# The fourth picked tile's v rows: one slot per fetch, tokens on partitions, summed by DVE

## The reference, cut to what matters

```
def peer_apply(h, expert, gate, u_tab, v_tab):
    # by blocks of tokens: h (n, 1024), expert and gate (n, 8, 16), tables (16384, 1024)
    ub = take(u_tab, expert)                  # one u row for each token and slot
    vb = take(v_tab, expert)                  # one v row for each token and slot
    a  = gelu(einsum('nd,nhkd->nhk', h, ub))  # 128 dot products a token
    return einsum('nhk,nhkd->nd', gate * a, vb)
# block(): x = x + gate2 * peer_apply(...), then a final rmsnorm with g_final
```

## Time and profile before

| | |
|---|---|
| time, median of 3 runs | 3561.27 us (3556.86 to 3562.12) |
| time of the profiled execution | 3564.63 us |
| its span, first to last instruction | 3563.0 us |
| mean granted TensorE clock | 0.949 |
| PE busy | 3114.4 us, 87% |
| DVE busy | 2311.0 us, 65% |
| POOL busy | 1446.0 us, 41% |
| ACT busy | 904.1 us, 25% |
| mixing on PE (L1742) in the chain that ended last | 7% |

### The profile page before, as it was taken

The page is one execution under the profiler, slowest core; times in us unless marked ns, Lnnn a source line. Parts: engine busy times, 40 slices in busy tenths (PEclk is TensorE's granted clock), DMA queues, the critical chain, the costliest instruction groups (busy, mean ns, idle before and its releaser), DMA issues.

```text
span 3563.0 us, 46587 instructions
## 1 busy us (share of the span) xinstructions
PE 3114.4 (87%) x17171; PEld 2346.7 (66%) x17171; DVE 2311.0 (65%) x4881; ACT 904.1 (25%) x1256; POOL 1446.0 (41%) x1188
## 2 busy tenths in 40 slices
PE   8899969444677557999999999999999999999996
PEld 1466634222454446888887888888888888888884
DVE  1233218999988976777776777776777775444445
ACT  0111111000666782222222122222222222221222
POOL 0001001555444556555554555555545543222224
PEclk9999989777899888999999999999999999999998
DMA  9611242666121329999998999999999997655654
GB/s 359 174 60 67 72 157 94 229 225 224 73 101 78 159 118 357 336 334 324 337 331 314 335 326 336 335 322 335 341 325 337 329 328 258 213 195 208 212 199 177
DMA packets 305763, 858.03 MB, mean 241 GB/s; under 512 B 25360, under 2 KB 108816, under 8 KB 303840
## 3 DMA queue, kind: packets, MB, share of 16 engines
q0 software_dynamic: 151344, 551.09, 43.0%
q1 hardware_dynamic: 154189, 305.27, 24.8%
q10 hardware_dynamic: 108, 0.22, 0.0%
HBM read 793.34 MB, written 63.15 MB: 240 GB/s over the span
## 4 chain that ended last, share of the span: by engine, by line
PE 59%; POOL 1%; issue 1%; DVE 1%; DMA 0%; ACT 0%; DVEq 0%
PE y_ps L1724 25%; PE a_ps L1705 24%; PE picked_ps L1742 7%; PE uT_ps L1692 3%; POOL shared L1446 0%; POOL rstd_d L1450 0%; DMA shared<-in_peer_u,ids 0%; POOL shared L1398 0%; POOL quad L1408 0%; DMA quad<-in_peer_v,idsT 0%; DVE h_lo L1640 0%; POOL quad L1446 0%; DVE uT_lo L1528 0%; DVE quad L1652 0%; DVE shared L1569 0%
## 5 line engine op out<-in xcount | busy, mean ns | idle before, releaser
L1408 POOL DMA_INDIRECT quad<-in_peer_v,idsT x512 | 533.4, 1042 | 518.2 <-PE picked_ps L1742 367.5
L1398 POOL DMA_INDIRECT shared<-in_peer_u,ids x384 | 444.5, 1158 | 640.5 <-DVE acts L1569 593.0
L1557 DVE TENSOR_TENSOR shared<-shared,y_ps 128x512 f32<-128x512 f32 x640 | 439.2, 687 | 340.2 <-PE y_ps L1724 312.1
L1705 PE MATMUL a_ps<-h_hi,uT_lo 128*128 128x320 f32 x2048 | 643.1, 314 | 1.7 <-DVE h_lo L1640 1.7
L1705 PE MATMUL a_ps<-h_hi,uT_hi 128*128 128x320 f32 x2048 | 633.1, 309 | 0.0
L1705 PE MATMUL a_ps<-h_lo,uT_hi 128*128 128x320 f32 x2048 | 633.1, 309 | 0.0
L1724 PE MATMUL y_ps<-v_hi,m_lo 128*128 128x512 f32 x1280 | 510.7, 399 | 11.0 <-DVE shared L1557 8.5
L1724 PE MATMUL y_ps<-v_lo,m_hi 128*128 128x512 f32 x1280 | 504.3, 394 | 0.0
L1724 PE MATMUL y_ps<-v_hi,m_hi 128*128 128x512 f32 x1280 | 501.6, 392 | 0.0
L1569 DVE CUSTOM_DVE_ANT_0 shared<-shared 128x1024 f32<-128x1024 f32 x384 | 464.6, 1219 | 22.3 <-DMA shared<-in_peer_u,ids 17.2
L1705 PEld LDWEIGHTS a_ps<-h_hi,uT_lo 128*128 128x128 f32 x2048 | 385.3, 188 | 7.2 <-issue 2.1
(11 more groups left out here) (172 smaller groups left out, 4220.1 us busy)
## 6 DMA issues: line engine op xcount, KB each, us to landing
shared<-in_peer_u SPq DMA_DIRECT2D x128, 512.0 KB
v_all<-in_peer_v SPq DMA_DIRECT2D x128, 512.0 KB
gate_blocks<-dense SPq DMA_DIRECT2D x10, 4096.0 KB, 11.7
gates<-gate_blocks SPq DMA_DIRECT2D x64, 640.0 KB
w_ada<-in_w_ada SPq DMA_DIRECT2D x12, 2048.0 KB, 11.0
x_in<-in_x_prompt SPq DMA_DIRECT2D x16, 512.0 KB, 4.1
quad<-in_peer_v,idsT POOLq DMA_INDIRECT x512
shared<-in_w_in SPq DMA_DIRECT2D x8, 768.0 KB, 12.5
```

Of the source, the lines that this page charges most:

```text
L1398: pool.indirect_dma_start(out=rows[n % 4], out_offset=None, in_=u_table, in_offset=bass.IndirectOffsetOnAxis(ap=ids[:, t, slot:slot + 1], ...
L1408: pool.indirect_dma_start(out=quads[half][q], out_offset=None, in_=v_table, in_offset=bass.IndirectOffsetOnAxis(ap=idsT[:, t, token:token ...
L1557: nc.vector.tensor_tensor(part, part, y_ps[n % RING][:, :], ALU.add).then_inc(S.y_free, 1)
L1705: last = nc.tensor.matmul(a_ps[n][:, 0:GROUP], lhs[s][:, k, :], rhs[:, k, tok], start=k == 0 and m == 0, stop=k == KD - 1 and m == 2)
```

## The change

For tile 3 alone (MIXED = 3 tiles are mixed as before) the v rows are fetched like the u rows: one slot of 128 tokens at a time, tokens on partitions, into the ring of four. DVE multiplies each by its token's weight (a column of mT, not transposed) and adds it to a sum in SBUF (add_row). POOL fetches no tokens and PE mixes nothing in the last quarter. ACT takes gelu from acts without PE's transpose, and the gates of tile 3 are kept untransposed in routing. FINAL becomes 0 to 8 in order. The buffers of the tail lie elsewhere, so that SP loads g_final, gate2, the three sums and the first two x1 tiles before the dense work is over.

```diff
--- before.py
+++ after.py
@@ -17,6 +17,7 @@
...
 PICKED = 4
+MIXED = PICKED - 1
@@ -876,7 +877,11 @@
                 act.wait_ge(S.slotsT_ps, t + 1)
                 nc.scalar.activation(idsT[:, t, :], x_ps[:, 0, :], ACT.Copy).then_inc(S.slotsT, 1)
-                nc.scalar.activation(gatesT[:, t, :], x_ps[:, 2, :], ACT.Copy).then_inc(S.slotsT, 1)
+                if t < MIXED:
+                    nc.scalar.activation(gatesT[:, t, :], x_ps[:, 2, :], ACT.Copy).then_inc(S.slotsT, 1)
+                else:
+                    nc.scalar.activation(gatesT[:, t, :], slots[:, 2, :, :].rearrange("p h k -> p (h k)"), ACT.Copy)\
+                        .then_inc(S.slotsT, 1)
             def left_rows(d, b):
@@ -1239,6 +1244,8 @@
     SEGMENT = PAIRS // PICKED
     PER_PAIR = P // SEGMENT
     DOTS = (PICKED - 1) * P
+    ROWS = DOTS + P
+    MIXED_PAIRS = MIXED * SEGMENT
     with ExitStack() as mem:
         ff, u, token_row, rows = expert_memory(shared)
         ids, idsT, gatesT, acts = picks
@@ -1263,20 +1270,20 @@
         mean = sbuf(nc, mem, "mean_d", [P, TILES])
         rstd = sbuf(nc, mem, "rstd_d", [P, TILES])
         h_raw = [ff[:, t, :] for t in range(DENSE)]
-        sums = quads[1][0]
-
-
-        x1 = [u[0], u[1], rows[0], rows[1]]
-        g_last = rows[2]
-        gate2 = [token_row, rows[3]]
+        sums, added = quads[1][0], quads[0][3]
+
+
+        x1 = [sums, token_row, u[0], u[1]]
+        g_last = quads[1][1]
+        gate2 = [quads[1][2], quads[1][3]]
         squares = uT_hi[1][:, :, :].rearrange("p k t -> p (k t)")
-        FINAL = [*range(PICKED - 1), *range(PICKED, TILES), PICKED - 1]
+        FINAL = range(TILES)
         def total(t):
             if t >= PICKED:
                 return ff[:, t - PICKED, :]
-            return sums if t == PICKED - 1 else quads[0][t]
+            return quads[0][t]
         u_loaded = [S.u0, S.u1]
         v_loaded = [[S.v00, S.v01], [S.v10, S.v11]]
         gates_loaded = [S.gates0, S.gates1]
@@ -1295,13 +1302,13 @@
         def pairs(eng, pair):
             for s in range(PICKED):
-                pair(s * SEGMENT, 0, s * SEGMENT // 2, opens=s)
+                pair(s * SEGMENT, 0, s * SEGMENT // 2, s, opens=s)
                 looped = SEGMENT // 2 - 1 - int(s == PICKED - 1)
                 with eng.Fori(0, looped) as i:
-                    pair(i * 2 + (s * SEGMENT + 1), 1, i + s * SEGMENT // 2)
-                    pair(i * 2 + (s * SEGMENT + 2), 0, i + (s * SEGMENT // 2 + 1))
+                    pair(i * 2 + (s * SEGMENT + 1), 1, i + s * SEGMENT // 2, s)
+                    pair(i * 2 + (s * SEGMENT + 2), 0, i + (s * SEGMENT // 2 + 1), s)
                 for c in range(looped * 2 + 1, SEGMENT):
-                    pair(s * SEGMENT + c, c % 2, (s * SEGMENT + c) // 2)
+                    pair(s * SEGMENT + c, c % 2, (s * SEGMENT + c) // 2, s)
         @block.sync
         def _(sp):
@@ -1329,7 +1336,7 @@
                     dst = y_sample.rearrange("b t d -> (b t) d")
                 sp.dma_start(dst, total(t)).then_inc(S.stored, 16)
-            def pair(c, parity, half, opens=None):
+            def pair(c, parity, half, s, opens=None):
                 last = isinstance(c, int) and c == PAIRS - 1
                 if opens is not None and 1 <= opens < PICKED - 1:
                     sp.wait_ge(S.used, opens * P)
@@ -1357,19 +1364,21 @@
             def load_x1(n):
                 sp.dma_start(x1[n % 4], x1_rows[FINAL[n], :, :]).then_inc(x1_loaded[n % 4], 16)
             x1_loaded = [S.x1_0, S.x1_1, S.x1_2, S.x1_3]
-            sp.wait_ge(S.used, DOTS)
+            sp.wait_ge(S.mixed1, MIXED_PAIRS)
             sp.dma_start(g_last, g_final.partition_broadcast(P)).then_inc(S.g_last, 16)
             sp.dma_start(gate2[0], mod_rows[0, GATE2, :].partition_broadcast(P)).then_inc(S.gate2_0, 16)
             for b in range(STREAMS):
                 sp.dma_start(gate2[1][b * STEP:(b + 1) * STEP, :], mod_rows[1 + b, GATE2, :].partition_broadcast(STEP))\
                     .then_inc(S.gate2_1, 16)
+            sp.wait_ge(S.sums_out, 16 * MIXED)
+            for t in range(MIXED):
+                sp.dma_start(total(t), sums_rows[t, :, :]).then_inc(sums_in[t], 16)
+            sp.wait_ge(S.used, DOTS)
+            for n in range(2):
+                load_x1(n)
             sp.wait_ge(S.uT_ps, EB + 1)
-            for n in range(4):
+            for n in range(2, 4):
                 load_x1(n)
-            sp.wait_ge(S.mixed0, PAIRS)
-            sp.wait_ge(S.sums_out, 16 * (PICKED - 1))
-            for t in range(PICKED - 1):
-                sp.dma_start(total(t), sums_rows[t, :, :]).then_inc(sums_in[t], 16)
             for n in range(TILES):
                 if n + 4 < TILES:
                     sp.wait_ge(S.summed, n + 1)
@@ -1388,15 +1397,15 @@
             pool.iota(column[:, :], pattern=[[1, 32]], base=0, channel_multiplier=0,
                       allow_small_or_imprecise_dtypes=True).then_inc(S.column, 1)
-            def fetch_u(n):
-
-                if n >= DOTS:
+            def fetch_row(n):
+
+                if n >= ROWS:
                     return
                 if n >= 4:
                     pool.wait_ge(S.used, n - 3)
-                t, slot = n // P + 1, n % P
+                t, slot = min(n // P + 1, PICKED - 1), n % P
                 pool.indirect_dma_start(
-                    out=rows[n % 4], out_offset=None, in_=u_table,
+                    out=rows[n % 4], out_offset=None, in_=u_table if n < DOTS else v_table,
                     in_offset=bass.IndirectOffsetOnAxis(ap=ids[:, t, slot:slot + 1], axis=0))\
                     .then_inc(row_loaded[n % 4], 16)
@@ -1412,17 +1421,17 @@
             def fetch_half(c, half, n):
-                if c and c < PAIRS:
+                if c and c < MIXED_PAIRS:
                     pool.wait_ge(mixed[half], c)
                 for step, q in enumerate((1, 2, None, 3, None, None, 0, None)):
                     if q is None:
-                        fetch_u(n)
+                        fetch_row(n)
                         n += 1
-                    elif c < PAIRS:
+                    elif c < MIXED_PAIRS:
                         fetch_v(c, half, q)
             for n in range(4):
-                fetch_u(n)
+                fetch_row(n)
             for q in (1, 2, 3, 0):
                 fetch_v(0, 0, q)
             pool.wait_ge(S.h_lo, DENSE)
@@ -1439,8 +1448,8 @@
                     t = FINAL[n]
                     if t >= PICKED:
                         pool.wait_ge(S.y_free, RING + (PAIRS - 1) * OUTPUTS + (t - PICKED) * 2 + 2)
-                    elif t == PICKED - 1:
-                        pool.wait_ge(S.sums, PICKED * 2)
+                    elif t >= MIXED:
+                        pool.wait_ge(S.used, ROWS)
                     else:
                         pool.wait_ge(sums_in[t], 16)
                     pool.tensor_tensor(total(t), total(t), gate2[int(t == TILES - 1)], ALU.mult)\
@@ -1482,16 +1491,20 @@
                     nc.scalar.activation(sums[:, n * HALF:(n + 1) * HALF], picked_ps[n][:, :], ACT.Copy)\
                         .then_inc(S.sums, 1)
-            def pair(c, parity, half, opens=None):
+            def pair(c, parity, half, s, opens=None):
                 if opens:
                     take_sums(opens - 1)
                 uT(c * 2 + 1, 1)
                 if not (isinstance(c, int) and c <= 1):
                     act.wait_ge(S.y_ps, (c - 1) * OUTPUTS)
                 gelu(c, parity, 0, 0)
-                if opens is not None:
+                if opens is not None and opens < MIXED:
                     act.wait_ge(S.turned, opens + 1)
                     nc.scalar.activation(mT[:, :], picked_ps[0][:, 0:P], ACT.Gelu).then_inc(S.slot_act, 1)
+                if opens == MIXED:
+                    act.wait_ge(S.used, DOTS)
+                    act.wait_ge(S.spread1, MIXED_PAIRS)
+                    nc.scalar.activation(mT[:, :], acts[:, :], ACT.Gelu).then_inc(S.slot_act, 1)
                 gelu(c, parity, 0, 1)
                 round_m(c, parity, 0)
                 if not (isinstance(c, int) and c == PAIRS - 1):
@@ -1508,7 +1521,6 @@
             for t in range(DENSE):
                 split_h(t)
             pairs(act, pair)
-            take_sums(PICKED - 1)
             for n in range(TILES):
                 act.wait_ge(S.summed, n + 1)
@@ -1559,9 +1571,10 @@
             def use(c, k):
                 n = c * PER_PAIR + k
+                t, slot = n // P + 1, n % P
                 if n >= DOTS:
+                    add_row(n, slot)
                     return
-                t, slot = n // P + 1, n % P
                 if slot == 0:
                     dve.wait_ge(S.row_in, t * 16)
                     dve.wait_ge(S.turned, t)
@@ -1570,6 +1583,18 @@
                                                scale=1.0, scalar=0.0, op0=ALU.mult, op1=ALU.add,
```

(25 more changed lines are left out.)

## The result

The changed kernel takes 3500.76 us (median of 5 runs, 3498.78 to 3505.46) against 3561.37 us (3556.86 to 3564.86): a ratio of 0.983, 95% interval 0.9819 to 0.984. Forecast was 3501 us. The profiled execution has 3505.46 us, a span of 3503.8 us and a mean granted clock of 0.946; it is 59.2 us shorter than the profiled execution of before.

The account below looks back on a forecast made before the run. PE was taken to bound the last quarter; 59.9 + 2.05 − 1.7 = 60.2 us saved, taking the profiled 3564.6 to 3504.4, or 3501 us after allowing 3.4 above the median; range 3492 to 3510, chance 0.80.

Parts of the forecast that it names:

- What bounds: Last quarter: PE sets the pair's length, 33.65 us, with DVE half idle and DMA time free.
- What leaves PE: Last quarter: two mixes a pair go, 3.99 us, so 33.65 becomes 29.66; 59.9 us for pairs 48 to 62.
- What comes to DVE: Last quarter: eight adds a pair at 1.28 us each, two spreads fewer, near 24 of 29.7 us busy; adds hidden.
- The second tight place: Middle of a pair: four outputs in a ring of two, the fifth needing the third's collect; priced at 0.
- the slack: End of a pair: time left between m_lo on DVE and PE's next outputs that need it, 0.45 us.
- The rival in which DVE sets the pace: Last quarter: m_lo comes late each pair, one to two us a pair lost, 3517 to 3533 us; chance 0.10.
- The slower rival, POOL's issues: Every add waits out one POOL fetch issue of 0.94 us, a pair takes 37.2 us, 3618 us; chance 0.06.
- The rows: Last quarter: 128 fetches by slot in a ring of four, tightest turn about 12 us, no waits; priced at 0.
- the rival: Last quarter: rows arrive late if a ring turn exceeds 14.8 us; at 16.8 no gain, 3561 us; chance 0.02.
- The last pair: Pair 63: loss of 1.7 us, bounds 1.2 and 6.0; last outputs 6.7 to 7.5 us after the previous pair's ninth output.
- the block: Pair 63: DVE held up by POOL's first two gate2 multiplications, up to 4.77 us, mostly caught up; taken as 0.5.
- The tail: From the start of the last outputs to the end: length unchanged, 51 us, paced by POOL and DVE in turn.

Follow-up runs that it names:

- experiment 1: Changed kernel with 16 matmuls of the mix's size, results unread, put back on PE at both mix places of each last-quarter pair: 3563.31 us, ratio 1.0002.
- experiment 3: Changed kernel with one extra 1.28 us DVE operation in pairs 49 to 61, behind the last add, before the second v_lo: 3514.1 us, ratio 0.987.
- experiment 4: Changed kernel with one extra 1.28 us DVE operation in pairs 49 to 61, behind the pair's fourth add: 3500.83 us, ratio 0.9834.
- experiment 7: Changed kernel with each tile 3 row fetch released one add later, as in a ring of three tiles instead of four: 3517.81 us, ratio 0.9882.
- experiment 2: Changed kernel without 127 of the 128 row fetches and adds of tile 3; only slot 0 fetched and multiplied: 3499.63 us, ratio 0.9828.
- experiment 6: Changed kernel in which POOL's first multiplication by gate2 waits for the last add, nothing else changed: 3503.29 us, ratio 0.9842.
- experiment 9: The changed kernel once more as it stands, on one chip with a repeat of another kernel: 3502.37 us, ratio 0.9841.
- experiment 5: Changed kernel, pair 63: both v_lo before the second weigh, last two adds after m_lo; POOL's second gate2 multiplication waits for them: 3496.03 us, ratio 0.982.
- experiment 8: Changed kernel with each tile 3 row fetch released two adds later, as in a ring of two tiles: 3583.94 us, ratio 1.0064.

## Why the prediction came out

**What bounds: right.** With PE's work put back, and nothing else, the time is the old one (experiment 1).

**What leaves PE: right, with the size a little low.** 4.12 us a pair instead of 3.99, 61.8 in 15 pairs instead of 59.9. By the rows of experiment 1 a middle mix costs 1.85 + 0.24 = 2.09 us (I had 2.05) and a last one 1.85 + 0.15 = 2.00 (I had 1.94): I counted the slower step of the outputs behind the middle mix, but not the same thing in the transposes behind the last one.

**What comes to DVE: right, and right in its place.** 1.28 us an add, 0.82 busy, 0.44 us of slack. One statement was wrong: two adds stand side by side in every pair, not only in pair 48. They take 2.67 us instead of some 2.5, at a place where nothing waits. The second tight place, four outputs in a ring of two, cost nothing either: 24 matmuls in 5.47 us. That the slack, not the sum, decides is shown by experiments 3 and 4. The rival in which DVE sets the pace is one more operation at the end of a pair away, and by experiment 3's price of 1.0 us a pair it would have come at the lower end of what I gave it.

**The slower rival, POOL's issues: fell.** From pair 48 to 3430 us no add is above 1.286 us, though 37 times an add ran while a fetch was issued, in issues of up to 1.93 us.

**The rows: right that they are in time, wrong in what limits them.** For the rival I compared the ring's turn with the average, 14.8 us, as if all rows took equally long. What counts is each row's own turn in DVE's uneven order against its own time to land. In the changed kernel the shortest turn is 11.9 us, as forecast, but for a row that lands within 5 us of its issue; the late row of each pair lands 8.6 to 10.2 us after its issue and has a turn of 12.9, so 2.4 to 4.0 us are left. One tile less and this row comes late, once a pair (experiment 7), long before the ring sets the pair. The DMA share rose to 0.72 instead of 0.67 without more bytes a second than expected (235 GB/s, 208 × 33.65 / 29.53 = 237); why is open.

**The last pair: right.** 7.28 us after the ninth output, forecast 6.7 to 7.5: 1.2 for the add in front of m_lo and 0.5 of the block, which does last as long as POOL. Experiment 2 shows that without the adds it would be 5.56. In experiment 1, whose longer pair lets DVE catch the block up (it waits 0.24 us in front of the second weigh), it is 3513.47 − 3506.71 = 6.76, so 1.2 for the add and 0.5 for the block are what each cost. The Trainium skill (SBUF — State Buffer, Who interferes with whom) has a DVE instruction with two SBUF inputs and one of GpSimd's that reads SBUF block each other for a whole instruction; the 6.00 us add agrees, and goes further, since it lasted through two of POOL's.

**The tail: the step that failed.** I gave it its old length, 51 us; it took 53.46. The first mean of the tail came 3460.65 − 3450.34 = 10.31 us after the last outputs began, and 3519.82 − 3511.89 = 7.93 before: the 2.4 us are lost by then, and twelve matmuls with steps of 0.43 instead of 0.23 are 2.4 us. The longer wait in front of the outputs cost not only itself but PE's clock behind it. The other traces bear this out: up to the thirteenth matmul of the last outputs the slower steps cost 1.29 us in experiment 6, 1.54 in experiment 1 and 2.38 in experiment 7, and the tails there took 52.40, 52.63 and 53.66 us, which is 1.29, 1.52 and 2.55 more than before.

The sum with the measured terms is 61.8 + 2.05 − 1.73 − 2.35 = 59.8. In the profiled execution pair 48's second first product began 0.73 us later (2981.55, 2980.82 before), which leaves 59.0; measured are 59.2. The changed kernel's second trace (experiment 9) has this product at 2975.76, 5.8 us earlier, and takes 3498.0 − 2975.76 = 522.24 us from there to its end, the first one 522.25, the kernel before 3563.0 − 2980.82 = 582.18: 59.9 us are the change's from pair 48 on, and single executions differ by several us ahead of it. So the forecast of 60.2 was as near as it was by luck: two errors of about 2 us, the pairs' gain and the tail's loss, cancelled. The terms that I gave for the range lead to 3493 and 3512, not 3492 and 3510; nothing turns on that. What stays open is what brings PE's clock down behind such a wait: the runs show that it follows, but the wait's length alone does not order them (below).

## What to carry to other kernels

Where an in-order engine takes over work, price it by place: find the instruction on which the bounding engine waits next, and count only what stands in front of it; the same 1.28 us cost nothing four places earlier and 1.0 us a pair there. Hold each row's turn in a ring, not the mean turn, against that row's own time from issue to landing: here one row of eight took twice as long as most. And put work that must come at the end of a loop behind what the next stage waits for: DVE's order in the last pair, with one POOL multiplication moved behind it, was worth 5.5 us.

## What the runs showed of the hardware

- PE's clock after a wait: in nine traces PE waited 1.99 to 6.26 us for m_lo in front of the last outputs, and behind it six to thirteen matmuls ran at the lower level (granted 0.50). Behind waits of 0.16 (experiment 5), 0.7 (experiment 3, its 13 pairs) and 0.80 us (before) none did. The length of the wait does not order the stretches: seven matmuls after 2.65 us (experiment 2), six after 5.99 (experiment 6), twelve after 4.37 and after 6.26 (experiment 8). Nor does the clock always fall at once: in experiment 4, after 4.35 us, three matmuls still ran at 0.99, and then eight at 0.50.
- An operation on DVE that meets one of POOL's multiplications takes 3.63 us beside 2.42 (experiment 5). One that meets two in a row waited for both in the changed kernel (6.00 us beside 4.78) and in experiments 1, 3, 4 and 7. In experiments 6 and 8, where POOL's first had begun during a v_lo, it waited for the first only: m_lo of experiment 6, 2.96 us, ended at 3445.69 + 2.96 = 3448.65, POOL's second at 3444.91 + 5.96 = 3450.87. POOL's issues of indirect fetches held no add up (1.286 us at most beside them).
- A row fetch of 512 KB lands 4.0 to 7.9 us after its issue begins for seven of the eight rows of a pair, and after 8.6 to 10.2 us for the eighth (changed kernel, pairs 50 to 61).
